# Even attention: high parts of the state-space outputs copied by GpSimd, and one panel of the gated units split two steps later

## The reference

```python
def even_layer(hn, ...):
    q, k, v, gate_a, u, gate_b = split_cols(hn @ w_in, EVEN_SPLITS)
    q = rms_norm(q, q_g); k = rms_norm(k, k_g)
    att = swa_sink_attention(q, k, v, sinks, rel_bias) * jax.nn.silu(gate_a)
    ssm = s5_mixer(u, ..., glu_w, glu_b) * jax.nn.silu(gate_b)
    return jnp.concatenate([att, ssm], axis=-1) @ w_out

def s5_mixer(u, ...):
    y = ...                      # state-space outputs, 1024 x 512
    y = jax.nn.gelu(y)
    h = y @ glu_w + glu_b        # "gated unit"
    return h[..., :W] * jax.nn.sigmoid(h[..., W:])
```

## Time and profile before

| | us |
|---|---|
| median of 3 runs | 2075.47 |
| lowest, highest | 2074.58, 2079.49 |
| the profiled execution | 2075.31 |
| its span, first to last instruction | 2074.1 |
| TensorE busy | 1991.6 (96%) |
| VectorE busy | 1413.2 (68%) |
| ScalarE busy | 870.4 (42%) |
| GpSimd busy | 652.3 (31%) |

### The profile page before, as it was taken

How to read it: one execution, slowest core, us unless ns; L and a number is a source line. 1 busy time by engine, 2 the same in 40 slices (tenths; PEclk the granted TensorE clock), 3 DMA queues, 4 the chain that set the end, 5 groups by cost and what they waited for, 6 DMA issues and landing times.

```text
span 2074.1 us, 24462 instructions
## 1 busy us (share of the span) xinstructions
PE 1991.6 (96%) x9260; PEld 1519.8 (73%) x9260; DVE 1413.2 (68%) x2158; ACT 870.4 (42%) x1523; POOL 652.3 (31%) x484
## 2 busy tenths in 40 slices
PE   8999989999999999899899999999999999999997
PEld 6778856787558777566688787888777667778785
DVE  7657677522379995354437699899997655794549
ACT  5343376333467841444322333444225444362431
POOL 3676521452101211454344000000004543235443
PEclk9999999999999999999999999999999999999999
DMA  6322340441501122211143201111142112465322
GB/s 263 127 66 75 89 147 21 162 152 68 147 21 42 41 91 77 84 43 41 56 148 112 82 33 61 55 57 61 56 148 92 62 46 100 170 201 215 111 85 109
DMA packets 72430, 197.93 MB, mean 95 GB/s; under 512 B 11182, under 2 KB 20559, under 8 KB 71800
## 3 DMA queue, kind: packets, MB, share of 16 engines
q1 hardware_dynamic: 72168, 196.35, 27.5%
q10 hardware_dynamic: 144, 0.00, 0.0%
HBM read 152.89 MB, written 46.71 MB: 96 GB/s over the span
## 4 chain that ended last, share of the span: by engine, by line
PE 61%; DVE 15%; ACT 4%; issue 3%; DMA 2%; POOL 2%; SPq 0%; DVEq 0%; ACTq 0%; POOLq 0%
PE psum L262 59%; DVE m L2918 3%; PE psum L265 3%; POOL m L307 2%; DMA m<-in_w 1%; DVE m L2939 1%; DVE m L2154 1%; ACT m L297 1%; DVE m L536 1%; DVE m L452 1%; DVE m L527 1%; DVE m L317 1%; DVE m L3110 1%; DVE m L3049 1%; DVE m L3113 1%
## 5 line engine op out<-in xcount | busy, mean ns | idle before, releaser
L262 PE MATMUL psum<-m,m 128*128 128x512 f32 (+8 forms) x8460 | 1908.0, 394 | 48.8 <-DVE m L2273 10.4
L262 PEld LDWEIGHTS psum<-m,m 128*128 128x128 f32 (+3 forms) x8460 | 1432.7, 186 | 494.4 <-issue 158.5
L307 POOL TENSOR_TENSOR m<-m,m 128x1024 fp32r<-128x1024 f32 (+1 forms) x122 | 308.6, 2534 | 990.0 <-ACT m L297 989.7
L297 ACT ACTIVATE m<-m 128x1024 fp32r<-128x1024 f32 (+2 forms) x166 | 173.5, 1049 | 354.2 <-PE psum L262 227.2
L2918 DVE SCALAR_TENSOR_TENSOR m<-m,m,m 128x1024 f32<-128x1024 f32 x240 | 310.2, 1294 | 6.2
L265 PE MATMUL psum<-m,m 128*128 128x128 f32 x784 | 111.1, 278 | 20.6 <-ACT m L2439 5.7
L265 PEld LDWEIGHTS psum<-m,m 128*128 128x128 f32 x784 | 90.5, 142 | 41.8 <-ACT m L1431 10.6
L2154 DVE TENSOR_SCALAR_CACHE_REDUCE m<-m,m 128x896 bf16<-128x896 f32 (+4 forms) x130 | 102.8, 848 | 1.1
L2273 DVE CUSTOM_DVE_ANT_0 m<-psum,m 128x128 f32<-128x128 f32 (+3 forms) x64 | 48.2, 754 | 55.4 <-POOL m L2476 23.6
L2476 POOL TENSOR_TENSOR m<-m,m 128x384 f32<-128x384 f32 (+5 forms) x48 | 72.2, 1526 | 11.5 <-DVE m L2273 10.5
L2368 ACT ACTIVATE m<-m,m 128x1024 bf16<-128x1024 f32 (+1 forms) x62 | 64.1, 1036 | 23.2 <-DVE m L2181 23.2
(11 more groups left out here) (303 smaller groups left out, 1621.1 us busy)
## 6 DMA issues: line engine op xcount, KB each, us to landing
m<-in_w SPq DMA_DIRECT2D x164, 512.0 KB, 3.4
scr_hscr<-m SPq DMA_DIRECT2D x4, 2048.0 KB, 6.6
m<-scr_hscr SPq DMA_DIRECT2D x4, 2048.0 KB, 10.7
scr_turned<-scr_strip SPq DMA_DIRECT2D x8, 575.5 KB, 12.2
m<-in_x SPq DMA_DIRECT2D x4, 1024.0 KB, 8.0
scr_gscr<-m SPq DMA_DIRECT2D x16, 256.0 KB, 4.0
m<-in_x SPq DMA_DIRECT2D x2, 2048.0 KB, 8.1
m<-scr_turned SPq DMA_DIRECT2D x8, 512.0 KB, 3.6
```

The lines of the kernel that those rows point to most:

```text
L262: return self.nc.tensor.matmul(out, lhsT, rhs, start=start, stop=stop, skip_group_check=True)
L297: k.nc.scalar.activation(k.hi[SLOT[i]][:, 0:kk * n], k.raw[i % 2][:, 0:kk * n], ACT.Copy).then_inc(*k.up("w_hi", i))
L307: k.nc.gpsimd.tensor_tensor(lo, raw, hi.bitcast(F32), ALU.subtract).then_inc(*k.up("w_lo", i))
```

## The change

The high parts of y are no longer copied by ScalarE in steps 5 to 8. GpSimd copies each of them itself (`tensor_copy`), waits for its own copy, and subtracts. Its copy takes over the two waits that ScalarE's had (panel gb3 done, Gelu done). And the panels of the gated unit no longer hang on the gates but on a table of their own: panel 20 (glu2) is split in step 3 of ScalarE instead of 1, panel 21 (glu3) stays in step 5, but behind the tanh of gate (7,1) instead of ahead of it. On SP panel 22 is loaded in step 2 instead of 0, and both loads stand behind the store of a gate instead of ahead of it.

```diff
+    def late_panel(self, i):
+        return {2: 6, 4: 7}.get(i)
...
 (scalar_even)
         if E.late_gate(i - 1):
             _, m, half = E.late_gate(i - 1)
-            if half:
-                act_panel(k, 14 + m)
             gate(m, half)
+        if E.late_panel(i - 1):
+            act_panel(k, 14 + E.late_panel(i - 1))
...
-        if i in E.y_steps:
-            m = E.y_steps.index(i)
-            act.wait_ge(*at("panel_done", PANEL_AT["gb3"]))
-            act.wait_ge(*at("y_gelu", m))
-            act_parts(k, E.in_turn(m), E.YH[:, m, :].rearrange("p (c j) -> p c j", j=8), "y_hi", m)
...
 (pool_even)
-        if E.late_gate(i) and E.late_gate(i)[2]:
-            pool_panel(k, 14 + E.late_gate(i)[1])
+        if E.late_panel(i):
+            pool_panel(k, 14 + E.late_panel(i))
         if i in E.y_steps:
             m = E.y_steps.index(i)
-            pool.wait_ge(*at("y_hi", m))
             yh, yl = (x[:, m, :].rearrange("p (c j) -> p c j", j=8) for x in (E.YH, E.YL))
+            pool.wait_ge(*at("panel_done", PANEL_AT["gb3"]))
+            pool.wait_ge(*at("y_gelu", m))
+            G.tensor_copy(yh, E.in_turn(m)).then_inc(*up("y_hi", m))
+            pool.wait_ge(*last("y_hi"))
             G.tensor_tensor(yl, E.in_turn(m), yh.bitcast(F32), ALU.subtract).then_inc(*up("y_lo", m))
...
 (sync_even)
             _, m, half = E.late_gate(i)
-            if half:
-                sp_panel(k, 16 + m)
             gate_out(m, half)
+        if E.late_panel(i):
+            sp_panel(k, 16 + E.late_panel(i))
```

## The result

| | before | after |
|---|---|---|
| median of 5 runs each, us | 2075.47 | 2087.29 |
| lowest to highest, us | 2074.58 to 2080.92 | 2084.27 to 2088.11 |
| profiled execution, us | 2075.31 (span 2074.1) | 2085.62 (span 2084.4) |

The change makes the kernel slower: ratio 1.0046, 95% interval 1.0029 to 1.0062, that is 6 to 13 us. The forecast was 2083.5 in 2076 to 2088.

A forecast was written before the change was run, and what follows sets the result against it. TensorE, busy for 96% of the span, bounds the kernel, with gaps only before 322 us. VectorE is 10.7 us late, less 2.6 regained, leaving 8.1: 2075.31 + 8.1 = 2083.4, stated as 2083.5, range 2076 to 2088.

The forecast's parts named there:

- The mechanism: Even layer's attention: each VectorE instruction over SBUF waits for one GpSimd instruction in a dense row; 8.1 us later, chance 0.52.
- Panel: Moving panel 20 to step 3 removes the clash at 273.81, gaining 2.1 us, of which 1.0 reaches what follows.
- The copy's price: Each strided GpSimd copy of y was taken as 1.7 us, between ends of 1.07 and 2.85.
- the rule of four: Four copies are added, so each us of a copy's price counts four times in the sum.
- The let-in instructions: VectorE instructions let in between GpSimd's stream for y lengthen it by 8 x 0.2 = 1.6 us, ending at 320.0.
- Nine turns: Nine GpSimd instructions each hold one VectorE instruction of units 5 to 7, making unit 6's first L1172 10.7 us late.
- Recovery: After GpSimd's stream, units 6 to 9 take 10.7 us instead of 13.27, regaining 2.6 us.
- From 322 on the same durations as before, shifted: Sign of being right: from 322 us TensorE has no gaps, so the rest moves as a block.
- Low parts of y: The gated unit's linear part, at about 332 us, finds the last low part ready since 320.
- VectorE is not held again and again: Rival: GpSimd's stream holds one VectorE instruction, then lets a whole group through; 5.5 us earlier, 2069.9; chance 0.18.
- The short copy: Rival: the mechanism holds, but GpSimd's copy of y is short, costing +5.6 us, 2081.0; chance 0.15.
- TensorE's clock: Rival: after idle times of 5 to 10 us TensorE recovers at 1.2 GHz, 6 us more, 2089.5; chance 0.08.

The follow-up runs named there:

- e1_panel: Kernel before with only the panel and its tanh moved, ScalarE still copying the high parts of y; ratio 1.0000 (0.9992 to 1.0009), stage +0.3 us.
- e7_one_panel: Kernel before with the panel moved and the four L1172 of a unit merged into one two-input instruction; ratio 0.9990 (0.9981 to 1.0000), stage -0.05 us.
- e2_y: Kernel before with only the high parts of y moved to GpSimd, the panel left in step 1; ratio 1.0052 (1.0037 to 1.0068), stage +9.6 us.
- e12_dve: Kernel before with the four subtractions for the low parts of y on VectorE, none on GpSimd; ratio 0.9996 (0.9987 to 1.0005), stage +1.3 us.
- e3_quarters: Changed kernel with each GpSimd copy and subtraction of y cut into four quarter instructions; ratio 1.0023 (1.0013 to 1.0034), stage +3.4 us.
- e9_two: Changed kernel with the high parts of tiles 0 and 2 copied by ScalarE again, 1 and 3 by GpSimd; ratio 1.0018 (1.0008 to 1.0028), stage +5.7 us.
- e10_late7: Kernel before with 38 tiny VectorE instructions added ahead of unit 6; ratio 1.0039 (1.0026 to 1.0052), stage +10.1 us.
- e4_memsets: Changed kernel with GpSimd writing zeros instead of copying and subtracting y, result incomplete; ratio 0.9976 (0.9966 to 0.9986), stage -4.8 us.
- e8_same: Kernel before, unchanged, profiled once more; ratio 0.9995 (0.9986 to 1.0004), stage +0.02 us.
- e11_late4: Kernel before with 19 tiny VectorE instructions added ahead of unit 6; ratio 1.0029 (1.0017 to 1.0040), stage +6.7 us.

## Why the prediction was right

**The mechanism was right, and so was the size in the stage; what comes behind the stage was not foreseen.** Forecast 8.1 us at unit 9, measured 329.92 - 322.58 = 7.3 in VectorE's rows and 7.2 in TensorE's. The median, 2087.29, lies 3.8 us above the 2083.5 of the forecast and 0.7 below the top of the range: the sum had nothing for what follows the stage, and that the range still held was partly luck. By its steps:

- *Panel.* The L1176 at 273.82 take 0.87 instead of 3.01, the wait of 2.27 is gone, and the subtraction in its new place runs from 283.79 (forecast 283.8) and holds L1163 for 1.10 at 285.08 (forecast 1.1 at 285.07). Panel 21 began at 296.97 instead of the forecast 297.4. That 1.0 of the 2.1 reaches what follows is right: unit 5's L1176 begin at 299.97 instead of 301.12, of e1_panel at 300.16. That this 1.0 is a gain of the kernel was wrong for the panel alone, where a grant of 1.2 GHz takes it back.
- *The copy's price.* Forecast 1.7, measured 1.93 to 2.05: mis-sized by some 0.28 on average, or 1.1 us by the rule of four. It is ScalarE's price for the same access, 1.98. The step that erred is "nearer to ScalarE's row": it should have been that row itself. The estimate of 0.85 from the Trainium skill (GPSIMD Engine Reference, section When to use GPSIMD) doesn't hold for this strided copy.
- *The let-in instructions.* I added 8 x 0.2 = 1.6 us to the stream for them. It took 319.10 - 299.65 = 19.45, and its eight durations sum to 19.3: they cost the stream next to nothing. This outweighs the error in the copy, so that the stream ends at 319.1 instead of 320.0: two errors of opposite sign, which is luck.
- *Nine turns.* The panel meets one, L1171; the first two pairs the four L1176 of unit 5; L1182 and L1158 run free beside the third copy, as forecast. The third subtraction holds L1165 of unit 7 for 2.86. The last pair then holds two L1176 of unit 6, not L1167 and one of them: L1171 came through at 314.21 in 0.15. So the group of unit 6 was done at 319.77, where the forecast had 320.0 + 1.14 = 321.1. This is the part of the count that was 1.4 too high.
- *Recovery.* 2.6 forecast; from 319.77 - 310.45 = 9.3 late to 7.3, it was 2.0. One step took 326.32 - 322.19 = 4.13 instead of 3.57, with TensorE at 1.2 GHz up to 324.7 (VectorE's L1182 at 323.81 waits 0.48 for an L262).
- *"From 322 on the same durations as before, shifted."* Wrong in the profiled execution: 7.2 late at 345 us, 10.3 at the end. Below.
- *Low parts of y.* They were ready at 319.1, and no wait of TensorE for GpSimd's y_lo appears.

**The rivals.** That VectorE is not held again and again fell by the 9.52 us. The short copy fell by 1.93. TensorE's clock was real but small in after: its two idle times of 9.0 and 4.85 us were each followed by transposes of 1.94 instead of 1.14, in stretches where TensorE waited anyway, so it cost 0.5 and not 6. Where it did matter was in places that I hadn't priced: behind waits of 1.7 to 2.3 us, at 1.5 us each, in e1_panel, e7_one_panel, e2_y and e12_dve, and behind a wait of over 3 us just ahead of the first full step, at 2.6 to 2.7 us, in e3_quarters and e9_two.

**What is behind the stage.** Of the 10.3 us at the end of after, 3.1 come behind 345 us. TensorE's lateness against before goes 7.4 at 819 us, 5.6 at 1185, 8.4 at 1390, 10.1 at 1598 and 10.3 at 2056. The windows of after (first) have a low grant at three places where those of before (second) have none:

```profile
1290.00:1300.00 10.00, 10.00 (x45) 8.09 (x44) 9.79 (x9) 1.63 (x2) 0.00 (x0) 0.83 0.14 54
1474.00:1484.00 10.00, 7.86 (x28) 6.04 (x27) 9.86 (x9) 0.00 (x0) 0.00 (x0) 0.83 0.32 105
1624.00:1634.00 10.00, 8.06 (x24) 4.48 (x23) 8.04 (x10) 4.62 (x13) 4.80 (x5) 0.83 0.05 20
```

```profile
1282.00:1292.00 10.00, 10.00 (x53) 8.31 (x52) 9.82 (x9) 1.63 (x2) 0.00 (x0) 1.00 0.14 54
1465.00:1475.00 10.00, 7.89 (x36) 6.19 (x35) 9.82 (x10) 0.00 (x0) 0.00 (x0) 1.00 0.29 105
1614.00:1624.00 10.00, 8.07 (x31) 5.08 (x30) 8.04 (x10) 4.50 (x13) 4.91 (x5) 1.00 0.05 18
```

and lacks one that before has, at 1150 us (0.90 there, 1.00 in after), which is the step from 7.4 down to 5.6. At the first of them TensorE is busy for all of the 10 us in both kernels and gets through 45 instead of 53 matmuls. So here the added time is the clock's. Whether the change causes it is another matter. e10_late7 is as late as after and has none of it; e3_quarters and e9_two have low grants near 1477 and 1627 us like after, with 4.7 and 5.2 us behind the stage, and yet their ratios give 1.4 us more and 2.0 less than their stages. Over the twelve kernels beside after, ratio less stage is between -2.1 and +1.4 us. My reading, which no run proves, is that these grants fall differently from execution to execution and are no regular part of the price; but each kernel was profiled once, so for after it stays open whether the 2.4 us between its stage (7.2) and its ratio (9.6, interval 6 to 13) are more than scatter.

## What to carry to other kernels

Where GpSimd and VectorE both work over SBUF, count instructions, not busy time: in a dense row of GpSimd's work each VectorE tensor_scalar or tensor_tensor on SBUF, tiny ones too, waits for one whole GpSimd instruction, so work moved there is dear if it closes the gaps between what is there already. If it must go there, cut it into small pieces (+7.2 became +3.4, of which 2.6 were TensorE's clock), or leave it where it spaces GpSimd's instructions out: against e4_memsets the four copies on ScalarE and the four spaced subtractions cost 4.8 us, the eight in one row 12.0. A gain of 1 us ahead of a stretch that TensorE bounds can be lost to one grant of its low clock, so look at the granted clock of the first full step behind the last wait before you credit or blame an edit: of the stage figures here, e1_panel, e7_one_panel, e2_y, e3_quarters, e9_two and e12_dve each hold 1.5 to 3 us of it.

## What the runs showed of the hardware

- Reading 128x1024 fp32 with a step of 128 elements takes about the same time on three engines: ScalarE's copy 1.98 us against 1.04 plain, VectorE's subtraction 1.95 against the 1.22 of a tensor_tensor without such a step (L1175 in e7_one_panel), GpSimd's copy 1.93 to 2.05 (no run has it plain). GpSimd's subtraction pays less for it: 2.85 against the 2.36 of a panel's.
- A MEMSET on GpSimd holds tensor_scalar on VectorE but not tensor_tensor: L1176 3.87 for four against L1163 and L1165 0.16 each, in the same row of MEMSETs (e4_memsets).
- Not held beside GpSimd's copies in after: RECIPROCAL over 128x4 (0.18 us at 299.76) and an operation that reads PSUM (L1182, 0.41 at 309.41).
- The same wait of 2.27 us at 277 to 279 us was followed by a granted clock of 1.00 in before, e8_same, e10_late7 and e11_late4, and of 0.72 in e2_y and e12_dve, which cost 1.5 us. What tells these executions apart isn't settled.
